# Loading the forget-gate bias rows and the prompt's decay rows by DMA in a two-layer decoder step

## The reference

```python
# prompt: c_k is the running sum of logf over the keys, per head
sc = jnp.einsum('bqhd,bkhd->bhqk', qi, k).astype(jnp.float32) * scale
sc = sc + ci[..., :, None] - c_k[:, :, None, :]
...
# sample: r_past is, per head and cached key, the sum of logf of all later cached keys
r_past = lax.cumsum(lf_past, axis=1, reverse=True) - lf_past
s_past = (jnp.einsum('bqhd,bkhd->bhqk', q, k_past).astype(jnp.float32) * scale
          + cq[..., :, None] + jnp.transpose(r_past, (0, 2, 1))[:, :, None, :])
```

## Time and profile before

| | |
|---|---|
| time, median of 3 runs | 2062.54 us (2060.16 to 2063.29) |
| the profiled execution, its own time | 2061.77 us |
| its span, first to last instruction | 2060.1 us |
| PE busy | 1828.9 us (89%) |
| DVE / ACT / POOL busy | 964.4 / 541.7 / 125.8 us |
| granted TensorE clock, mean | 0.942 |
| DMA, mean over the span | 109 GB/s |

### The profile page before, as it was taken

One profiled execution on the slowest core, in us unless ns is written; L12 is line 12 of the kernel. 1 busy time (PEld: TensorE's weight loads), 2 busy tenths in 40 slices (PEclk: granted clock), 3 DMA queues, 4 the chain that ended last, 5 costly groups with the idle time before them and its releaser, 6 DMA issues.

```text
span 2060.1 us, 36026 instructions
## 1 busy us (share of the span) xinstructions
PE 1828.9 (89%) x13959; PEld 1588.1 (77%) x13959; DVE 964.4 (47%) x1532; ACT 541.7 (26%) x901; POOL 125.8 (6%) x267
## 2 busy tenths in 40 slices
PE   5999565899999999799877898988979899999998
PEld 4876434889999999799754555555549799999997
DVE  5397875443333222477554655566533533333222
ACT  3211223232222211243321333333322322222110
POOL 1000000000000000244210000000000000000000
PEclk9999866999999999999986999999989999999999
DMA  3211121222222322223352577777862122223221
GB/s 116 62 42 31 31 88 47 76 62 82 83 84 84 94 85 76 67 67 79 99 173 65 161 246 245 246 246 256 266 220 82 57 83 84 83 82 93 75 84 60
DMA packets 239464, 224.68 MB, mean 109 GB/s; under 512 B 12114, under 2 KB 199588, under 8 KB 239354
## 3 DMA queue, kind: packets, MB, share of 16 engines
q1 hardware_dynamic: 229168, 200.83, 31.9%
q0 software_dynamic: 8768, 19.09, 2.9%
q10 hardware_dynamic: 1418, 3.29, 0.5%
HBM read 215.37 MB, written 7.80 MB: 108 GB/s over the span
## 4 chain that ended last, share of the span: by engine, by line
PE 77%; DVE 14%; ACT 4%; issue 2%; DMA 1%; ACTq 0%; SPq 0%; DVEq 0%; POOL 0%
PE ps L1461 55%; PE ps L1816 4%; PE ps L1651 3%; PE ps L1832 2%; PE ps L1863 2%; PE ps L1443 1%; DVE tmp L419 1%; PE ps L1837 1%; DVE yc L698 1%; PE ps L1907 1%; DVE aL L423 1%; DVE prob L921 1%; DVE rb L429 1%; DVE rb L414 1%; PE ps L1923 1%
## 5 line engine op out<-in xcount | busy, mean ns | idle before, releaser
L1461 PE MATMUL ps<-aH,wH 128*128 128x288 f32 x2224 | 488.1, 301 | 50.0 <-DVE aL L423 34.5
L1461 PE MATMUL ps<-aL,wH 128*128 128x288 f32 x2224 | 480.9, 298 | 0.0
L1461 PE MATMUL ps<-aH,wL 128*128 128x288 f32 x2224 | 480.8, 298 | 0.0
L1461 PEld LDWEIGHTS ps<-aH,wH 128*128 128x128 f32 x2224 | 362.7, 191 | 59.3 <-issue 35.6
L400 DVE TENSOR_TENSOR wL<-raw,wH 128x1024 fp32r<-128x1024 f32 (+1 forms) x179 | 232.0, 1296 | 339.2 <-ACT wH L1063 336.1
L1461 PEld LDWEIGHTS ps<-aH,wL 128*128 128x128 f32 x2224 | 363.0, 191 | 0.0
L1461 PEld LDWEIGHTS ps<-aL,wH 128*128 128x128 f32 x2224 | 363.0, 191 | 0.0
L1063 ACT ACTIVATE wH<-raw 128x1024 fp32r<-128x1024 f32 (+1 forms) x179 | 199.0, 1112 | 409.2 <-PE ps L1461 359.6
L1461 PE MATMUL ps<-gH,wH 128*128 128x288 f32 x704 | 151.9, 297 | 4.8 <-DVE gL L616 4.8
L1461 PE MATMUL ps<-gH,wL 128*128 128x288 f32 x704 | 151.6, 296 | 0.0
L1461 PE MATMUL ps<-gL,wH 128*128 128x288 f32 x704 | 151.6, 296 | 0.0
(11 more groups left out here) (302 smaller groups left out, 1916.4 us busy)
## 6 DMA issues: line engine op xcount, KB each, us to landing
kring<-in_cache_fox_k_dram SPq DMA_DIRECT2D x128, 384.0 KB, 3.8
vring<-in_cache_fox_v_dram SPq DMA_DIRECT2D x128, 384.0 KB, 4.0
raw<-in_w_gate_up_dram SPq DMA_DIRECT2D x88, 512.0 KB, 3.7
raw<-in_w_down_dram SPq DMA_DIRECT2D x32, 704.0 KB, 4.5
raw<-in_fox_w_in_dram SPq DMA_DIRECT2D x21, 512.0 KB, 3.9
raw<-in_w_out_dram SPq DMA_DIRECT2D x16, 512.0 KB, 3.7
raw<-in_conv_w_in_dram SPq DMA_DIRECT2D x14, 512.0 KB, 3.8
raw<-in_w_mem_kv_dram SPq DMA_DIRECT2D x8, 512.0 KB, 3.6
```

Of the source, the lines that this page charges most:

```text
L1461: mm = nc.tensor.matmul(ps[:, 2 * slot + h, 0:HT], weights[:, w], a[:, k0 + k, h * HT:(h + 1) * HT], start=(first and k == 0 and weights i ...
```

## The change

Bias rows. The products that made `rtok` now make the bias with the page on the partitions and the key along the row: per head one product of `lfT` and `after`, and one small product `later` times `lftot` for the sums of later pages, which DVE adds while it copies, into `rrow`. POOL stores `rrow` to a tensor in HBM, and then loads, for each sequence, the rows of all 12 heads into the 96 rows of `S`, each row eight times. DVE's copy of the scores adds what lies in S. `rx`, POOL's copies and the PE products of L1837 are gone.

Decay rows. SP issues two DMAs per head pair, which read a row of `ncT` and write it to all 128 partitions of `ncb`. The PE products of L1899, the copies of ACT and DVE and their visits to PSUM bank 2 are gone.

```diff
@@ DVE
+            bank = group()
+            nc.vector.tensor_copy(rsum[:], bank[:, 0:NH]).then_inc(tr_free, 1)
+            dve.wait_ge(tr_free, tr[0])
             for g in range(NH // 4):
                 bank = group()
-                nc.vector.tensor_copy(rtok[:, 4 * g:4 * g + 4, :].rearrange("p h n -> p (h n)"), bank).then_inc(tr_free, 1)
+                nc.vector.tensor_tensor(rrow[:, 4 * g:4 * g + 4, :], bank.rearrange("n (h p) -> n h p", h=4),
+                                        rsum[:, 4 * g:4 * g + 4].unsqueeze(2).broadcast_to([NB * NP, 4, PG]), ALU.add).then_inc(tr_free, 1)
...
-            def decay(hp):
-                dve.wait_ge(xb_ready, VISITS["decay", hp, 1] + 1)
-                nc.vector.tensor_copy(ncb[:, 1, :], ps[:, 2, :]).then_inc(xb_free, 1)
...
                 if t == 0:
-                    dve.wait_ge(xb_free, VISITS["decay", hp, 1] + 1)
+                    dve.wait_ge(decay_in, 32 * (hp + 1))
...
-                if c == 0 and b >= 2:
-                    dve.wait_ge(yg_ready, p_group(b - 2, 3) + 1)
-                moved = nc.vector.tensor_scalar(S[b % 2][:, c * KEYS:(c + 1) * KEYS], ps[0:ROWS, 6 + k % 2, 0:KEYS],
-                                                stat[0:ROWS, at_:at_ + 1], None, ALU.add)
+                if c == 0:
+                    dve.wait_ge(r_in[b % 2], 16 * (b // 2 + 1))
+                s = S[b % 2][:, c * KEYS:(c + 1) * KEYS]
+                moved = nc.vector.scalar_tensor_tensor(out=s, in0=ps[0:ROWS, 6 + k % 2, 0:KEYS], scalar=stat[0:ROWS, at_:at_ + 1],
+                                                       in1=s, op0=ALU.add, op1=ALU.add)
@@ PE
+            nc.tensor.matmul(out[:, 0:NH], later[:], lftot[:], start=True, stop=True).then_inc(tr_ready, 1)
...
-                    nc.tensor.matmul(out[:, h * P:(h + 1) * P], after[:], lfT[:, 4 * g + h, :], start=True, stop=False)
-                    mm = nc.tensor.matmul(out[:, h * P:(h + 1) * P], lftot[:, 4 * g + h:4 * g + h + 1].broadcast_to([P, P]), later[:],
-                                          start=False, stop=True)
+                    mm = nc.tensor.matmul(out[:, h * P:(h + 1) * P], lfT[:, 4 * g + h, :], after[:], start=True, stop=True)
...
-                for pp in range(CPG):
-                    for j in range(3):
-                        r = rx[:, K_, pp, 4 * j:4 * j + 4, :].rearrange("p h q -> p (h q)")
-                        mm = nc.tensor.matmul(ps[QR * j:QR * j + QR, bank, pp * P:(pp + 1) * P], r, ident[:],
-                                              start=False, stop=(pp == CPG - 1), skip_group_check=True, tile_position=(0, QR * j))
...
-            def decay(hp, e):
...
@@ SP
+            def decay(hp):
+                if hp:
+                    sp.wait_ge(at_max, U0 + TT * hp)
+                for e in range(2):
+                    sp.dma_start(ncb[:, e, :], ncT[2 * hp + e:2 * hp + e + 1, :].unsqueeze(1).broadcast_to([1, P, SEQ])).then_inc(decay_in, 16)
...
             for m in range(RING):
                 if m == RING - 1:
                     sp.wait_ge(tr_free, marks["far"])
+                    decay(0)
                 values(m)
             for k in range(-1, TICKS):
                 if k + 1 + RING < CHUNKS:
                     keys(k + 1 + RING)
+                for hp in range(1, HP):
+                    if START[TT * hp - 1] + 2 == k:
+                        decay(hp)
                 if k >= LAG and k - LAG + RING < CHUNKS:
                     values(k - LAG + RING)
@@ POOL
-            pool.wait_ge(tr_free, marks["rtok"])
-            for k in range(CHUNKS):
-                if k >= 2:
-                    pool.wait_ge(sc_ready, k - 1)
-                r = rtok[:, :, CPG * k:CPG * k + CPG].rearrange("p h n -> p n h")
-                nc.gpsimd.tensor_copy(rx[:, k % 2], r.unsqueeze(3).broadcast_to([P, CPG, NH, NQ])).then_inc(rx_done, 1)
+            pool.wait_ge(tr_free, marks["rrow"])
+            for b in range(NB):
+                pool.dma_start(r_dram[b].rearrange("h (n p) -> n h p", p=PG), rrow[NP * b:NP * (b + 1)]).then_inc(r_out, 16)
+            pool.wait_ge(r_out, 16 * NB)
+            for b in range(NB):
+                if b >= 2:
+                    pool.wait_ge(yg_ready, p_group(b - 2, 3) + 1)
+                pool.dma_start(S[b % 2][:, 0:NPAST], r_dram[b].unsqueeze(1).broadcast_to([NH, NQ, NPAST])).then_inc(r_in[b % 2], 16)
```

More of the change, by code:

```diff
@@ L135, in units_at @@
         return [u for u in range(len(FOX_UNITS)) if START[u] + stage == k]
-    def heads_at(k, stage):
-        return [hp for hp in range(1, HP) if START[TT * hp - 2] + stage == k]
     def k_group(n, g):
@@ L146, in visits_early @@
     def visits_early(k):
-        return ([("out", u) for u in units_at(k, 4)] + [("decay", hp, 1) for hp in heads_at(k, 5)]
-                + [("probT", u, 0) for u in units_at(k, 3)])
+        return [("out", u) for u in units_at(k, 4)] + [("probT", u, 0) for u in units_at(k, 3)]
     def visits_late(k):
-        return [("probT", u, 1) for u in units_at(k, 3)] + [("decay", hp, 0) for hp in heads_at(k, 4)]
+        return [("probT", u, 1) for u in units_at(k, 3)]
     OUT_AT = [next(k for k in range(NCH * (b + 1) + LAG, TICKS + 2) if not visits_late(k)) for b in range(NB)]
     assert OUT_AT[-1] == TICKS
-    VISITS = {("decay", 0, 0): 0, ("decay", 0, 1): 1}
+    VISITS = {}
     for k in range(TICKS + 1):
@@ L275, in build @@
         ncx, o = at("ncx", [NS, NH, NQ], o)
-        rx, o = at("rx", [P, 2, CPG, NH, NQ], o)
-        rtok, _ = at("rtok", [P, NH, NB * NP], o)
+        r_dram = nc.dram_tensor("r_rows", [NB, NH, NPAST], F32).ap()
+        rrow, _ = at("rrow", [NB * NP, NH, PG], o)
+        rsum, _ = at("rsum", [NB * NP, NH], dw_at + 4 * NB * NP)
         lfrow, o = at("lfrow", [NB * NP, PG * NH], o)
         later, _ = at("later", [NB * NP, NB * NP], dw_at)
-        assert NB * NP <= KC * W
+        assert NB * NP + NH <= KC * W
         lftot, o = at("lftot", [NB * NP, NH], o)
@@ L367, in build @@
         e_done, zab_done, c_ready, c_done, stage_done = (sem(n) for n in ("e_done", "zab_done", "c_ready", "c_done", "stage_done"))
-        qx_done, lftot_done, rx_done = (sem(n) for n in ("qx_done", "lftot_done", "rx_done"))
+        qx_done, lftot_done = sem("qx_done"), sem("lftot_done")
+        r_in = [sem(f"r_in{p}") for p in range(2)]
+        r_out, decay_in = sem("r_out"), sem("decay_in")
         yg_ready, yg_v, yg_a = (sem(n) for n in ("yg_ready", "yg_v", "yg_a"))
@@ L886, in _ @@
             dve.wait_ge(tr_free, tr[0])
+            bank = group()
+            nc.vector.tensor_copy(rsum[:], bank[:, 0:NH]).then_inc(tr_free, 1)
+            dve.wait_ge(tr_free, tr[0])
             for g in range(NH // 4):
                 bank = group()
-                nc.vector.tensor_copy(rtok[:, 4 * g:4 * g + 4, :].rearrange("p h n -> p (h n)"), bank).then_inc(tr_free, 1)
-            marks["rtok"] = tr[0]
+                nc.vector.tensor_tensor(rrow[:, 4 * g:4 * g + 4, :], bank.rearrange("n (h p) -> n h p", h=4),
+                                        rsum[:, 4 * g:4 * g + 4].unsqueeze(2).broadcast_to([NB * NP, 4, PG]), ALU.add).then_inc(tr_free, 1)
+            marks["rrow"] = tr[0]
             prob, pT = mb1["prob"], mb1["pT"]
@@ L1002, in _ @@
             begin(0)
-            decay(0)
             for g in range(3):
@@ L1015, in _ @@
                     prompt_out(u)
-                for hp in heads_at(k, 5):
-                    decay(hp)
                 if k < CHUNKS:
@@ L1340, in keys_T @@
                                          ACT.Copy).then_inc(yg_a, 1)
[L1342 to L1346, removed]
             def prompt_exp(u):
@@ L1410, in _ @@
                     prompt_exp(u)
-                for hp in heads_at(k, 4):
-                    decay(hp)
                 if c == 0 and 1 <= b <= NB:
@@ L1793, in _ @@
             pe.wait_ge(lftot_done, 1)
+            out = ps[:, 6 + tr[0] % 2, :]
+            tr[0] += 1
+            nc.tensor.matmul(out[:, 0:NH], later[:], lftot[:], start=True, stop=True).then_inc(tr_ready, 1)
             for g in range(NH // 4):
@@ L1824, in sample_scores @@
                 pe.wait_ge(yg_v, (G + 1) // 2)
-                pe.wait_ge(rx_done, k + 1)
                 if c == 0:
@@ L1831, in sample_scores @@
                     for j in range(3):
-                        nc.tensor.matmul(ps[QR * j:QR * j + QR, bank, 0:KEYS], qx[:, q, 2 * j + odd, :], kT[:, K_, 2 * j + odd, :],
-                                         start=(odd == 0), stop=False, skip_group_check=True, tile_position=(0, QR * j))
-                for pp in range(CPG):
-                    for j in range(3):
-                        r = rx[:, K_, pp, 4 * j:4 * j + 4, :].rearrange("p h q -> p (h q)")
-                        mm = nc.tensor.matmul(ps[QR * j:QR * j + QR, bank, pp * P:(pp + 1) * P], r, ident[:],
-                                              start=False, stop=(pp == CPG - 1), skip_group_check=True, tile_position=(0, QR * j))
```

(8 more changed lines are left out.)

## The result

The changed kernel takes 2121.67 us (median of 4, 2121.36 to 2122.70) against 2061.35 us before (median of 4, the three of the table above and one more): ratio 1.0295 [1.0277, 1.0313], slower. The profiled execution took 2121.72 us, 60.0 more than that of before (2061.77). The forecast was 2106 us, slower, with 2012 to 2140 as the range.

What follows compares the result with a forecast made beforehand. PE was taken to bound the cached-key stage (89% busy). From 2061.8 us: start +1, bias and decay products -45.1, waits for rows +73.5, clock +14.6, giving 2106 us, 2.1% slower; range 2012 to 2140.

Steps and rivals of the forecast that it cites:

- start (first score copy): Before the cached-key stage: stores and first S load put the first score copy at 1134.2 against 1133.39, +1 us.
- bias products: PE's L1837 products in 64 ticks removed: between 20.8 and 34.6 us saved, middle 27.7 taken.
- decay products: Two PE products per head pair removed, with bank and copy waits, five pairs: 17.4 us saved.
- waits for the rows: VectorE at each pair's first maximum waits for two one-partition transfers: 14.7 us, five times, 73.5 us.
- clock: PE runs at granted clock 0.50 after each of five stalls, 2.9 us each: +14.6 us.
- the slot: Time from the keys' issue until a pair's rows are needed: 13.3 us, less 5.4, leaving 7.9.
- (a): Rival: 16 engines read the one partition side by side, rows land inside 7.9 us; 2018 us, chance 0.25.
- (b): Rival: rows overlap or a partition gives twice the share, 9.6 us a pair, stall 5.1; 2050 us, chance 0.07.
- the chain's 5.5%: Share of the bias products in the steady stretch's chain of waits: 20.8 of 379 us, the lower estimate.
- the first pair's rows cost nothing: Pair 0's decay rows, issued before the values loads of 1110.46, two ticks before use, add 0 us.
- the stated bound of +14: Upper bound for the start's delay, if its transfers take twice as long; +1 us was taken.
- What would show it: Signs: ncb transfers over 19 us, five VectorE waits over 10, PE idle 75 more, clock 0.50, ticks 0.5 shorter.

Runs made afterwards that it cites:

- experiment 1: Kernel before with only the bias rows moved to DMA, decay rows still made on PE: 2063.36 us, ratio 1.0004.
- experiment 3: Changed kernel with the decay rows stored once to HBM and read from there instead of from one SBUF partition: 2048.59 us, ratio 0.9934.
- 6: Kernel before with only the decay rows by DMA, read from HBM; bias products stay on PE: 2036.29 us, ratio 0.9885.
- experiment 5: Changed kernel with decay rows from HBM, first two sequences' bias rows stored first and first S load halved: 2041.57 us, ratio 0.9908.
- 4: Changed kernel with pairs 1 to 4 reading decay rows from 4 neighbouring, 4 spaced, 16 and 128 SBUF partitions: one run, 2083.8 us.
- experiment 7: Changed kernel with a second decay-row buffer, rows still from one SBUF partition but issued eight ticks earlier: 2121.49 us, ratio 1.0293.
- 8: Changed kernel with two decay-row buffers and issue eight ticks ahead, pairs 1 to 5 issued by GpSimd: 2116.64 us, ratio 1.0259.

## Why the prediction was right, and where its terms were off

The direction and the cause were right. The working by terms, with what the stages show:

| term | predicted | measured |
|---|---|---|
| start (first score copy) | +1 | +14.5 |
| bias products | -27.7 | -9.8 (experiment 1) |
| decay products | -17.4 | -17.7 (3 against 1), -17.6 (6) |
| waits for the rows | +73.5 | +58.4 |
| clock | +14.6 | +14.6 (PE's busy time, the change against 3) |
| late loads and the rest | not in the sum | +1.1 |
| sum | +44 | +61.1, and -1.2 behind the stage |

- **Waits for the rows: right in kind, 15 us too large.** A row goes at some 28 GB/s, 9.4 us; 9.6 was predicted, from a sixteenth of the fullest bin of the earlier trace rows. No row of before showed such a read, so that pace was a guess that came out. After the keys' issue the second row lands in 20.9 to 22.1 us, 21.5 in the mean of the five pairs (22.6 predicted): the 3.4 us for the keys in front was added whole, but the first row lands 11.8 to 12.9 us after its own issue, so some 2 to 3 us are left for it. The larger part of the error is the slot, from the keys' issue to VectorE being ready: 8.1 us in the first of these pairs, but 9.9 in the mean (7.9 predicted), since it shrank by 3.4 us and not by the 5.4 that were taken off. So the waits are 10.3 to 12.9 us instead of 14.7. Rivals (a) and (b) fall: the rows neither land in the slot nor overlap.
- **Decay products: right**, to 0.3 us, stalls for the bank and VectorE's copy included. Experiments 3 and 6 have this gain without the transfers' price.
- **Bias products: the step that failed most in the stage.** Between 0.54 us in every tick and the chain's 5.5% I took the middle, 27.7. Even the lower of the two, 20.8, was too much: the chain's share says where PE was last, not how soon another engine would be. Only 33 of 63 ticks lose some 0.44 us; in experiment 1 half of the busy time that PE saved came back as idle time (10.2 of 20.1). Part of the saving is lost to the start: behind the stop there PE runs at clock 0.52 to 1146. From the fourth tick on the bias part saves 13.2 us, and 12.4 over the stage by experiment 5 against 6, where the stop is shorter.
- **The start: the step "the first pair's rows cost nothing" failed.** I asked only when they are needed and not what they hold up. rrow stood at 1120.89 (1119.9 predicted) and the stores' issue ended at 1125.9, as predicted; but they landed by 1138.25 instead of 1128.2, 10.0 us late, behind pair 0's reads. The first load then took 9.7 us instead of 6.0, 3.7 late. Without those reads the start costs 5.5 (experiment 1). The 14.5 us lie at the stated bound of +14, for another reason than the one I gave it.
- **The clock: right, the match to a tenth by luck.** Behind the first stall 5 us at 0.50 and 2 at 0.65 are seen; behind each of the other four the first 7 us are at 0.50. In these PE is busy 1.4 to 4.0 us, less than the 5.85 taken from the earlier trace rows, and full speed is back only 7 to 12 us after the wait. Values came late as predicted, but of the 15.7 us they cost little: PE's waits for values are 11.9 us, in experiment 3 10.7.
- **What would show it** came as said: five waits of over 10 us at the maximum, rows at 21 us for a pair, clock 0.50 behind, PE idle in the stage 66 us more (75 predicted), score copy 478 ns as before. Between the stalls a tick is shorter by 0.44 us only in half of them (0.5 in all was the sign). The sign for a wrong start came too: the first score copy at 1147.91, far from 1134.

The errors partly cancelled: the start and the bias products gave 31 us too little, the waits 15 too much. The time fell inside the range, 15.7 us above the forecast; but the range went down to 2012 for rival (a), so the time alone would have fitted quick rows as well. What bears out the mechanism are the five waits and experiments 3, 4, 7 and 8.

## What to carry to other kernels

Before a row is repeated by DMA, look at where its source lies: 128 reads of one SBUF partition go at what it and its neighbours share (here some 28 GB/s), while the same row read from HBM lands like any other load. A slow transfer must be priced by what it holds up, not only by when its own data are due: here issuing it earlier or from another queue only moved the same stop to the next load. And a PE saving counts only in the ticks that PE itself bounds; so compare tick lengths, and do not go by the share of a chain.

## What the runs showed that was not expected

- A 256 KB read of one partition keeps the DMA engines about 9 tenths busy at some 28 GB/s in total, and other loads stand behind it: 8.8 us for SP to issue two loads of values, stores of 96 KB landing after 10.6 us instead of 2.8.
- Four neighbouring partitions as the source are no better than one (15.37 us of wait), four partitions four apart nearly free (1.82 us).
- S's loads, 768 KB each read from HBM with every row repeated 8 times, take 9.7 us in the change (8.8 in experiment 1, 10.8 in experiment 7), against 6.3 for 1024 KB of ks. Why was not tried.
